# A two-block transformer kernel: second layer norm and final norm by token columns with sums made ahead, merge gates ahead of the wait for the attention outputs, up chunks three tiles behind

## What is computed

```python
# first block
proj = (layer_norm(x) * (1 + sc1) + sh1) @ w_in             # q, k, v of two attentions, two gates
merged = sigmoid(gate_a) * (o_a @ w_br_fox) + sigmoid(gate_c) * (o_c @ w_br_chunk)     # merge1
x = layer_norm(alpha * x + (1 + g1) * (merged @ w_out), ln1_g, ln1_b)                  # out1, LN_1
h = layer_norm(x) * (1 + sc2) + sh2                                                    # LN_MID
a, val = split(causal_conv3(h @ w_up))                                                 # up1
x = layer_norm(alpha * x + (1 + g2) * ((silu(a) * val) @ w_down), ln2_g, ln2_b)        # down1, LN_2
# second block, on 16 meta tokens and the 512
h = h + 0.5 * swiglu(rmsnorm(h, ffn1_norm), ...)                                       # RMS_1, up2, down2
u = rmsnorm(h, mix_norm) @ w_in_2                                                      # RMS_MIX, back
h = h + (sigmoid(gate_a) * (ya @ w_branch_att) + sigmoid(gate_b) * (yb @ w_branch_gla)) @ w_out_2  # merge2, out2
h = h + 0.5 * swiglu(rmsnorm(h, ffn2_norm), ...)                                       # RMS_2, up3, down3
return rmsnorm(h, final_norm)[:, 16:]                                                  # RMS_OUT
```

## Time and profile before

| | us |
|---|---|
| median of three executions | 2050.61 |
| the profiled execution | 2054.59 |
| its span in the trace | 2051.5 |
| TensorE busy | 1966.9 |
| VectorE busy | 1027.1 |
| ScalarE busy | 717.8 |
| mean granted TensorE clock | 0.984 of full |

### The profile page before, as it was taken

One profiled execution on the slowest core, in us unless ns is written; L12 is line 12 of the kernel. 1 busy time (PEld: TensorE's weight loads), 2 busy tenths in 40 slices (PEclk: granted clock), 3 DMA queues, 4 the chain that ended last, 5 costly groups with the idle time before them and its releaser, 6 DMA issues.

```text
span 2051.5 us, 26743 instructions
## 1 busy us (share of the span) xinstructions
PE 1966.9 (96%) x10897; PEld 1661.6 (81%) x10897; DVE 1027.1 (50%) x1409; ACT 717.8 (35%) x957; POOL 23.8 (1%) x45
## 2 busy tenths in 40 slices
PE   5899999998999999989999999999999999999997
PEld 3787887885788888779999999878878888888885
DVE  7688753446555542274443423776344454444323
ACT  3454443324555532162222222545323242222212
POOL 0100000000000000000000000000000000000000
PEclk9899999999999999999999999999999999999999
DMA  7543313231222222312222222211122222222221
GB/s 274 204 156 134 124 42 125 82 103 42 102 82 102 96 71 98 104 42 88 96 82 96 71 98 94 94 42 42 62 83 82 103 82 102 87 97 89 85 98 55
DMA packets 34847, 195.44 MB, mean 95 GB/s; under 512 B 3680, under 2 KB 3696, under 8 KB 19552
## 3 DMA queue, kind: packets, MB, share of 16 engines
q1 hardware_dynamic: 29008, 173.55, 24.1%
q0 software_dynamic: 5776, 21.02, 3.1%
HBM read 192.46 MB, written 2.10 MB: 95 GB/s over the span
## 4 chain that ended last, share of the span: by engine, by line
PE 89%; DVE 7%; issue 1%; ACT 1%; DMA 1%; SPq 0%; DVEq 0%; ACTq 0%
PE PS L638 88%; DVE W_lo L1757 1%; DMA A_low<-in_wada 1%; PE PS L795 1%; DVE A_high L2414 1%; DMA ring<-in_wada 0%; DVE ring L2414 0%; DVE INV L1816 0%; DVE PT_lo L1854 0%; DVE N L1821 0%; ACT H_hi L1290 0%; DVE stats L1839 0%; DVE X L2446 0%; ACT T L1290 0%; DVE stats L2038 0%
## 5 line engine op out<-in xcount | busy, mean ns | idle before, releaser
L638 PE MATMUL PS<-H_hi,W_hi 128*128 128x512 f32 (+1 forms) x1976 | 632.0, 354 | 31.6 <-DVE H_lo L1804 12.4
L638 PE MATMUL PS<-H_hi,W_lo 128*128 128x512 f32 (+1 forms) x1976 | 633.8, 355 | 0.0
L638 PE MATMUL PS<-H_lo,W_hi 128*128 128x512 f32 (+1 forms) x1976 | 631.7, 353 | 0.0
L1757 DVE TENSOR_TENSOR W_lo<-W_raw,W_hi 128x2048 fp32r<-128x2048 f32 (+2 forms) x170 | 353.1, 2077 | 318.8 <-ACT W_hi L1290 318.5
L1290 ACT ACTIVATE W_hi<-W_raw 128x2048 fp32r<-128x2048 f32 (+2 forms) x170 | 295.6, 1739 | 376.3 <-PE PS L638 375.2
L638 PEld LDWEIGHTS PS<-H_hi,W_hi 128*128 128x128 f32 x1976 | 349.9, 191 | 89.8 <-issue 23.3
L638 PEld LDWEIGHTS PS<-H_hi,W_lo 128*128 128x128 f32 x1976 | 349.4, 191 | 49.7 <-issue 0.4
L638 PEld LDWEIGHTS PS<-H_lo,W_hi 128*128 128x128 f32 x1976 | 348.8, 190 | 50.0 <-issue 0.2
L638 PE MATMUL PS<-G_hi,W_lo 128*128 128x512 f32 (+1 forms) x704 | 210.7, 340 | 0.0
L638 PE MATMUL PS<-G_hi,W_hi 128*128 128x512 f32 (+1 forms) x704 | 210.5, 340 | 0.0
L638 PE MATMUL PS<-G_lo,W_hi 128*128 128x512 f32 (+1 forms) x704 | 210.2, 339 | 0.0
(11 more groups left out here) (300 smaller groups left out, 2036.2 us busy)
## 6 DMA issues: line engine op xcount, KB each, us to landing
W_raw<-in_wts SPq DMA_DIRECT2D x119, 1024.0 KB, 4.8
W_raw<-in_wdown SPq DMA_DIRECT2D x48, 704.0 KB, 4.1
ring<-in_wada POOLq DMA_DIRECT2D x32, 512.0 KB, 3.8
A_high<-in_wada SPq DMA_DIRECT2D x6, 1024.0 KB, 18.4
A_low<-in_wada SPq DMA_DIRECT2D x2, 1024.0 KB, 10.9
X<-in_xT SPq DMA_DIRECT2D x2, 1024.0 KB, 10.4
X<-in_xT POOLq DMA_DIRECT2D x1, 2048.0 KB, 8.9
out<-N SPq DMA_DIRECT2D x8, 256.0 KB, 2.1
```

The costliest lines, as they stand in the source:

```text
L638: return nc.tensor.matmul(*a, **kw)
L1757: vector.tensor_tensor(W_lo[:, c.odd, 0:size], W_raw[:, c.odd, 0:size], W_hi[:, c.odd, 0:size].bitcast(FP32), ALU.subtract).then_inc(w_lo, 1)
```

## The change

1. **merge1, merge2.** The waits ahead of `merge_one` are gone. The first gate chunk waits for group 0 by `group_free` in `project`, and for group 1 only before its second feature tile (bank 2). The waits for the attention outputs stand before the first branch chunk.
2. **up1.** `pair_up` runs chunk 1 three tiles behind chunk 0 (PAIR_LAG = 3); the first projections keep LAG = 2.
3. **LN_2** becomes `column_norm`. During down1 VectorE keeps a running sum of tiles 0 to 5 in `SQ[:, 0]` (five additions of 128x512). The mean is that sum and tiles 6 and 7: three products in place of eight, in bank 1, with no wait for the PSUM groups. The variance uses 32 columns of `inv_d`, even tiles to partitions 0 to 31 and odd tiles to 32 to 63 of bank 6. Then come the steps known from LN_1: copy of 64 rows, turn, copy to `SC`, one addition of the two halves, root and reciprocal on 128x4, spread to bank 7.
4. **RMS_OUT** becomes `out_norm`. Before the last residual VectorE adds the squares of tiles 1 to 6 into `SQ[:, 0]` (six additions). The statistic is made with the squares as weights and one column of `inv_d` as data, four products for the sum (ahead of the last tile) and four for tile 7, so it comes out as token columns; root and reciprocal on 128x4; spread to bank 7; the scaling reads it from PSUM.

```diff
+PAIR_LAG = 3
+PAIR_COLUMNS = 9
+PRESUMMED = {"out1": 0, "down1": 5, "down3": 10}
...
-                for kt in range(KT + LAG):
+                for kt in range(KT + PAIR_LAG):
...
-                    if kt >= LAG:
-                        last = tile(1, kt - LAG)
+                    if kt >= PAIR_LAG:
+                        last = tile(1, kt - PAIR_LAG)
...
+            def column_norm(n, after):      # TensorE
+                pe.wait_ge(sem("presummed"), PRESUMMED["down1"] + KT - 3)
+                mm(PS[:, 1, :], inv_d[:, :], presum(), start=True, stop=False)
+                for k in (KT - 2, KT - 1):
+                    wait_src(pe, n, k)
+                    last = mm(PS[:, 1, :], inv_d[:, :], n.src(k), start=False, stop=k == KT - 1)
+                last.then_inc(n.sem("mean"), 1)
+                for g in range(2):
+                    pe.wait_ge(psum_free[g], after[g])
+                for k in range(KT):
+                    pe.wait_ge(*n.reach("squared", k + 1))
+                    r = 32 * (k % 2)
+                    last = mm(PS[r:r + 32, 6, :], inv_d[:, 0:32], SQ[:, k, 0:SEQ], start=k < 2, stop=k >= KT - 2, skip_group_check=True)
+                last.then_inc(n.sem("variance"), 1)
+                pe.wait_ge(sem("norm_rows"), 2)
+                for blk in range(NB):
+                    last = nc.tensor.transpose(PS[:, 5, blk * HEAD:(blk + 1) * HEAD], ST[:, blk * P:(blk + 1) * P], ident[0:HEAD, 0:HEAD])
+                last.then_inc(sem("norm_turned"), 1)
+                pe.wait_ge(sem("norm_column"), PAIR_COLUMNS + 3)
+                spread(C_INV1).then_inc(sem("norm_spread"), 1)
+            def out_norm():                 # TensorE
+                n = RMS_OUT
+                pe.wait_ge(sem("presummed"), PRESUMMED["down3"] + KT - 2)
+                pe.wait_ge(psum_free[0], st["down3"].held[0] + KT // 2)
+                for blk in range(NB):
+                    mm(PS[:, blk, 0:1], SQ[:, 0, blk * P:(blk + 1) * P], inv_d[:, 0:1], start=True, stop=False)
+                pe.wait_ge(*n.reach("squared", KT))
+                for blk in range(NB):
+                    last = mm(PS[:, blk, 0:1], SQ[:, KT - 1, blk * P:(blk + 1) * P], inv_d[:, 0:1], start=False, stop=True)
...
                         k = 2 * mp
-                        project(s, At(s.c + k, 4, i), At(k, 4, i), SEQ, META)
+                        project(s, At(s.c + k, 4, i), At(k, 4, i), SEQ, META,
+                                before_second=lambda: pe.wait_ge(psum_free[1], s.held[1]))
...
+                        if mp == 0:
+                            outputs_ready()
...
-            s = st["merge1"]
-            pe.wait_ge(psum_free[0], s.held[0])
-            pe.wait_ge(psum_free[1], s.held[1])
-            pe.wait_ge(sem("f_olo"), HEADS)
...
+            def add_to_presum(i, m):        # VectorE, after each residual of down1
+                if isinstance(i, int) and i == 0:
+                    if m == 1:
+                        vector.tensor_tensor(presum(), LN_2.src(0), LN_2.src(1), ALU.add).then_inc(sem("presummed"), 1)
+                elif not isinstance(i, int):
+                    dve.wait_ge(sem("presummed"), i * 2 + (PRESUMMED["down1"] + m - 1))
+                    x = X[:, bass.ds(i * 2 + m, 1), META:TOK].rearrange("p o t -> p (o t)")
+                    vector.tensor_tensor(presum(), presum(), x, ALU.add).then_inc(sem("presummed"), 1)
```

More of the change, by code:

```diff
@@ L393, in count @@
                     return PAIR_COUNTS[self.number - 1].get(what, 0)
+                if self.number == 3 and what == "inverse":
+                    return 0
                 if what in ("mean", "centred") and not self.center:
@@ L1269, in _ @@
             down("down1", SEQ, HIDDEN["up1"])
-            norm(LN_2, st["up2"].held)
+            column_norm(LN_2, st["up2"].held)
             project_late("up2", FH, RMS_1, TOK, 0)
@@ L1284, in _ @@
             down("down3", SEQ, HIDDEN["up3"])
-            norm(RMS_OUT, [st["down3"].held[g] + KT // 2 for g in range(2)])
+            out_norm()
         @block.scalar
@@ L2229, in body @@
                     b = At(k if tiles_per_batch == 2 else k // 2, 2, i)
+                    if name == "down3" and k == 3 and isinstance(i, int):
+                        out_squares()
                     used(At(s.c + k, step, i))
@@ new lines, in out_squares, with column_norm @@
+            def out_squares():
+                for k in range(1, KT - 1):
+                    dve.wait_ge(*RMS_OUT.reach("squared", k + 1))
+                    if k > 1:
+                        dve.wait_ge(sem("presummed"), PRESUMMED["down3"] + k - 1)
+                    vector.tensor_tensor(SQ[:, 0, 0:SEQ], SQ[:, 0, 0:SEQ], SQ[:, k, 0:SEQ], ALU.add).then_inc(sem("presummed"), 1)
+            def column_norm(n, after_tile):
+                dve.wait_ge(*n.reach("mean", 1))
+                for k in range(KT):
+                    vector.tensor_tensor(n.centred(k), n.src(k), PS[:, 1, :], ALU.subtract).then_inc(n.sem("centred"), 1)
+                dve.wait_ge(*n.reach("variance", 1))
+                vector.tensor_copy(ST[:, :], PS[0:HEAD, 6, :]).then_inc(sem("norm_rows"), 1)
+                dve.wait_ge(sem("norm_turned"), 2)
+                vector.tensor_copy(SC[:, C_MEAN:C_POWER + 1, :].rearrange("p (h c) b -> p h c b", h=2), turned()
+                                   ).then_inc(sem("norm_column"), 1)
+                dve.wait_ge(sem("norm_column"), PAIR_COLUMNS + 1)
+                vector.tensor_tensor(SC[:, C_VAR1, :], SC[:, C_VAR1, :], SC[:, C_MEAN, :], ALU.add).then_inc(sem("norm_column"), 1)
+                dve.wait_ge(*n.reach("deviation", 1))
+                vector.reciprocal(SC[:, C_INV1, :], SC[:, C_DEV1, :]).then_inc(sem("norm_column"), 1)
+                dve.wait_ge(sem("norm_spread"), 4)
+                for k in range(KT):
+                    vector.scalar_tensor_tensor(out=N2[:, k, 0:SEQ], in0=n.centred(k), scalar=n.gain(k), in1=PS[:, 7, :],
+                                                op0=ALU.mult, op1=ALU.mult).then_inc(n.sem("scaled"), 1)
+                    if k >= 3:
+                        after_tile(k - 3)
+                for k in range(KT - 3, KT):
+                    after_tile(k)
@@ new lines, in out_norm @@
+            def out_norm():
+                n = RMS_OUT
+                dve.wait_ge(*n.reach("deviation", 1))
+                vector.reciprocal(SC[:, C_INV1, :], SC[:, C_DEV1, :]).then_inc(n.sem("inverse"), 1)
+                dve.wait_ge(sem("norm_spread"), 5)
+                for k in range(KT):
+                    vector.scalar_tensor_tensor(out=N2[:, k, 0:SEQ], in0=n.src(k), scalar=n.gain(k), in1=PS[:, 7, :],
+                                                op0=ALU.mult, op1=ALU.mult).then_inc(n.sem("done"), 1)
```

83 lines of the change are left out of this document (56 added, 27 removed).

## The result

| | before | after |
|---|---|---|
| median | 2051.76 (2050.46 to 2054.67, 4 executions) | 2029.98 (2029.02 to 2032.68, 4 executions) |
| the profiled execution | 2054.59 | 2029.02 |
| its span | 2051.5 | 2027.0 |
| TensorE, VectorE, ScalarE busy | 1966.9, 1027.1, 717.8 | 1955.4, 1028.8, 717.5 |
| mean granted clock | 0.984 | 0.987 |

The ratio is 0.9895, 95% interval 0.9879 to 0.991: 21.8 us less. The forecast was 2029.0, with a sum of 21.8 us.

What follows compares the result with a forecast made beforehand. TensorE, busy 96% of the span, was taken as the bound, so its waits and needless work count. 4.4 + 0 + 1.65 + 8.0 + 0 + 7.7 = 21.8 us off the median 2050.61 gave 2029.0, range 2025.5 to 2034.0.

Steps and rivals of the forecast that it cites:

- merge1: Start of merge1: the 2.79 us wait on `O_lo` goes, and 1.65 us of low clock after it; 4.4 us gained.
- merge2: Start of merge2: the 1.65 us wait stays, since the gate chunk itself needs bank 0 released; 0 gained.
- up1: Up1's loop starts as before, its wait halves, and the low clock behind it goes; 1.65 us gained.
- LN_2: Second norm, between down1 and up2: three terms on TensorE's path, together 8.0 us gained.
- (a): Mean of LN_2: six instructions instead of 16, only the last two needing the last residual; 5.4 us gained.
- (c): LN_2 from the sums to the first scaled tile: 3.3 to 3.5 us instead of 4.15; 0.65 us gained.
- (b): Variance of LN_2: narrow products to alternating partition groups overlap and end 1.02 us behind the last square; 1.95 us gained.
- Sums made ahead: Eleven VectorE additions in down1 and down3, about 0.67 us each, are covered by idle time; 0 cost.
- Final norm: End of the kernel, last square to first scaled tile, 10.74 us before: 7.7 us gained, bounds 6.0 and 8.2.
- The clock came back: Rival: low clock near merge1 and up1 appears even without the waits; gain 18.5, time 2032.1 us; 18%.
- The small steps: Rival: narrow products do not overlap and final-norm hand-overs are long; gain 17.8, time 2032.8 us; 12%.
- The slower one: Rival: TensorE without pauses is granted less clock in dense stretches; 2068 us at 0.98; 5%, of which 3 end slower.

Runs made afterwards that it cites:

- g_turned: Changed kernel with merge2's first gate chunk making its bank 2 feature tile before its bank 0 one; 2031.59 us, ratio 0.9889 to the kernel before.
- b_lag: Kernel before with only the three-tile lag in up1 added; 2050.83 us, ratio 0.9988 to the kernel before.
- f_same: Changed kernel with LN_2's 32-column variance sums all going to partitions 0 to 31 instead of alternating; 2032.83 us, one execution.
- c_ln2: Kernel before with only the new LN_2 added; 2043.62 us, ratio 0.9955 to the kernel before.
- k_after: Changed kernel as it is, run again as base for the kernels beside it; 2031.25 us, ratio 0.9889 to the kernel before.
- l_lag2: Changed kernel with up1's lag put back from three tiles to two; 2032.56 us, ratio 0.9896 to the kernel before.
- h_fill: Changed kernel with unread filler products in the gaps of LN_2 and the final norm; 2025.54 us, ratio 0.9859 to the kernel before.

## Why the prediction was right, point by point

**merge1, forecast 4.4: 4.6.** The two terms are in the trace as such. From 325.29 (328.06 before) to the first gate product it is 2.60 us instead of 5.55, so 2.95 for the wait. From there to LN_1 it is 138.37 instead of 140.04, so 1.67 for the clock. Both covers held. `W_lo` of the branch chunk is ready before its turn, and `O_lo` ends at 330.4.

**merge2, forecast 0: 0.28.** The wait stayed, ended by the release of the last batch of the back, as the bank numbers said; `g_turned` shows that it is this bank. The 0.28 come from the wait becoming 1.37; which of the waits taken away from its front cost them was not tried.

**up1, forecast 1.65: 1.55 in the trace of `b_lag` and in that of the result, 0 against others.** The step "the loop starts as before" is exact: 29.43 in all fourteen traces (29.42 to 29.44). That the gain is the clock alone is right too. What failed is the certainty of the term. I took the low clock behind a 2.8 us wait as its price, and it comes in three traces of five. Three fifths of 1.55 make a value of about 0.9 us on average, an estimate from five traces, not 1.65.

**LN_2, forecast 8.0: 7.6 to 8.1.** (a) The six instructions end at 860.49, and VectorE starts on `N` behind them. Terms (a) and (c) together are 5.9 (7.85 less 1.97), against 6.05. (b) is 1.97 against 1.95. The step "alternating groups overlap" was read from LN_1 and is what `f_same` isolates. The Trainium skill has the rule of a drain at a change of tiling, TensorEngine Tiling (Array Packing), Key Properties, from which the prediction made about 1 us for (b). That doesn't follow, and LN_2 can't test the rule: TensorE has stood idle for 1.53 us when the first narrow sum starts and stands idle for 0.78 us behind the last one, so a drain at either change would lie in idle time. The sums end 1.11 us behind the last square, with a last pair of 1.02. Where changes do fall into work, in the attention of the changed kernel, a product of 128 columns on the whole array is followed by one on 64 rows 0.20 us after its start, and by one of its own kind 0.11 us after; what part of the 0.09 us is a drain isn't shown. In (c) I had taken 0.98 us for eight spreads; they take 1.16 at full clock and 1.38 to 2.08 where the low clock reaches them (1.66 in the profiled execution). That is the only term of LN_2 that was mis-sized, by 0.2 to 1.1: from the last sum to the first scaled tile it is 3.94 us in the profiled execution, where some 3.4 were forecast. The low clock behind the norm was left as it is in the forecast, and it stayed: 884.5 to 895 before, 869.5 to 880.5 after. More of it is busy time now, and the work lost by it is 3.23 us instead of 2.27. About 0.5 of this are the spreads, counted already; the other 0.4 are given back in up2, inside the bound of 0.5.

**Sums made ahead, forecast 0: 0.** VectorE's additions in down1 take 0.69 us each, no wait on `W_lo` appeared, and the stretch from up1's loop to the end of down1 has the same length with them (`c_ln2`).

**Final norm, forecast 7.7: 6.8, and up to 7.5 in repeats.** The step that was mis-sized is the spreads: 2.08 us at half the clock instead of 0.98; the lower bound of 6.0 contained that case, and the chosen value did not. With the same code the low clock begins later in some traces: the spreads take 1.46 us in `k_after` and 1.39 in `l_lag2`, and the first scaled tile starts 3.34 and 3.26 us behind the last square instead of 3.96. With fillers, spreads at 1.16, it is 3.04 (`h_fill`), the 3.0 that was forecast. Root, reciprocal and hand-overs take 0.54 us from the end of the load at 2016.30 to the spreads at 2016.84, against 0.7. The Trainium skill, ScalarE: Activation LUTs, What ACT_TABLE_LOAD costs, puts a drain of 1380 ns on each switch. The trace contradicts it: the square ends at 2015.00, the load takes 1.28 us from 2015.02, and the root starts at 2016.31.

**The sum.** 4.6 + 0.3 + 1.6 + 7.6 + 6.8 = 20.9, and from the mark on the traces differ by 21.8. Terms that no step named make the difference. LN_1's 24 spreads fell under the low clock and took 4.28 us instead of 2.94, which costs 1.0; 0.4 are lost behind LN_2; and the back gives 2.4, because the kernel before has three stretches of low clock there and this one a single one. That these cancel is chance: `k_after` has three of them again and still takes 1907.0 us from the mark to the end, since LN_1 (15.46 against 16.49), LN_2 (362.13 against 362.65) and the final norm (3.34 against 3.96) met less of the low clock in it. The terms of the edits were right to within 1 us each, and the total is closer than they are.

**The rivals.** The clock came back in merge1, always. The small steps did not eat the rest. merge2's wait stayed. The slower one, a lower grant in dense stretches, is refuted by 344 and 418 us at 1.00. That the profiled execution of before lay 4.0 us above the median, which made me take the sum off the median, is explained in part: the front alone, with equal code, varies by 4 us (120.1 to 124.1), and its low-clock stretches shift with it; and 3.1 us of that execution lie outside its span, where the one after has 2.0.

## What to carry to other kernels

Read which buffer ends a wait before moving the wait: two equal edits gave 4.6 us and 0.3 us, told apart by a bank number. When a stage of small dependent steps is cut short, price its TensorE products at the low clock, not at the full one, unless something keeps the engine busy; where a bank is idle, unread products there were worth 1.8 to 3.1 us, with two norms at stake. Before crediting an edit with a clock term, look whether kernels without the edit show it too: the lag's 1.55 us came without the lag in two of five traces. And in these sums narrow products saved time only when the next one went to other columns.

## What the runs showed of the hardware

- A norm of dependent small steps had a low clock within it or right behind it: eight 128-column spreads took 1.16 us at full clock and 2.08 at the low one. Up2's first products ran at the low clock in the eleven traces without fillers in LN_2 and at 1.00 in the three with them.
- Where TensorE waits for tiles, the low clock costs nothing: seven microseconds at 0.51 in up1 changed the start of the loop by 0.00 us.
- Equal waits of 2.8 us had a low clock behind them in three traces of five; the back, with the same code, shows one, two or three stretches of it.
- Sixteen instructions with weights of 32 columns took 7.03 us into one group of partitions and 5.14 into two in turn, where they waited for the squares.
- A load of ScalarE's tables took 1.28 us, and in the final norm 1.31 us lie in all between the end of the square and the start of the root.
